# Two transformer blocks on one core: seven additions for one strided sum, operand tiles ahead of a weight split, and waits bank by bank

## The reference, cut to what matters

```python
def rms_norm(x, g):
    xf = x.astype(jnp.float32)
    y = xf * lax.rsqrt(jnp.mean(xf * xf, axis=-1, keepdims=True) + EPS)
    return (y * g.astype(jnp.float32)).astype(x.dtype)
...
    ca = memory_cross_attention(rms_norm(x, g_mem_pre[l]), m, ...)     # mem_q
    x = x + rms_norm(swiglu(rms_norm(x, g_ffn_pre[l]), ...), ...)      # ffn_up
...
    mix = dilated_attention_mixer(rms_norm_2(x, mixer_norm[layer]), ...)   # dil_in, dil_out
    x = x + mix
    x = x + conv_ffn(rms_norm_2(x, ffn_norm[layer]), ffn_w_up[layer], ...) # conv_up
```

## Time and profile before

| | us |
|---|---|
| median of 3 runs | 1588.36 |
| lowest and highest | 1587.85, 1592.78 |
| the profiled execution | 1588.06 |
| its span (first to last instruction) | 1586.2 |
| TensorE busy | 1538.0 (97%) |
| VectorE busy | 865.1 (55%) |
| ScalarE busy | 610.0 (38%) |
| GpSimd busy | 244.8 (15%) |

### The profile page before, as it was taken

One profiled execution on the slowest core, in us unless ns is written; L12 is line 12 of the kernel. 1 busy time (PEld: TensorE's weight loads), 2 busy tenths in 40 slices (PEclk: granted clock), 3 DMA queues, 4 the chain that ended last, 5 costly groups with the idle time before them and its releaser, 6 DMA issues.

```text
span 1586.2 us, 21184 instructions
## 1 busy us (share of the span) xinstructions
PE 1538.0 (97%) x7444; PEld 1270.7 (80%) x7444; DVE 865.1 (55%) x1135; ACT 610.0 (38%) x911; POOL 244.8 (15%) x273
## 2 busy tenths in 40 slices
PE   6999999999999999999999899999999999999998
PEld 4888777987887788888888678888997888888887
DVE  6213777436462743433423776747877766667323
ACT  6322433544234422222322643434765433334222
POOL 0010000014102400000000455645451100000000
PEclk9999999999999999999999999999999999999999
DMA  5343000431203133333223122232102232332331
GB/s 163 116 150 106 1 1 0 160 128 59 80 1 106 54 106 106 88 98 106 85 101 106 54 73 87 82 105 80 28 1 80 80 106 83 102 105 80 106 106 53
DMA packets 152797, 132.04 MB, mean 83 GB/s; under 512 B 6300, under 2 KB 137628, under 8 KB 152740
## 3 DMA queue, kind: packets, MB, share of 16 engines
q1 hardware_dynamic: 150836, 128.11, 26.3%
q0 software_dynamic: 848, 3.17, 0.6%
q10 hardware_dynamic: 1056, 0.00, 0.0%
HBM read 129.15 MB, written 2.12 MB: 83 GB/s over the span
## 4 chain that ended last, share of the span: by engine, by line
PE 89%; DVE 5%; ACT 2%; POOL 2%; issue 1%; DMA 0%; DVEq 0%; ACTq 0%; SPq 0%; POOLq 0%
PE ps L1715 25%; PE ps L1717 25%; PE ps L1716 25%; PE ps L1938 3%; PE ps L438 2%; PE ps L2048 1%; POOL x_t L743 1%; DVE work L1245 1%; PE ps L471 1%; DVE a_lo L1266 1%; PE ps L1926 1%; PE ps L573 1%; PE ps L1955 1%; PE ps L2035 1%; PE ps L1869 1%
## 5 line engine op out<-in xcount | busy, mean ns | idle before, releaser
L1715 PE MATMUL ps<-a_hi,w_hi 128*128 128x512 f32 (+2 forms) x1672 | 652.5, 390 | 15.9 <-DVE a_lo L1266 8.9
L1717 PE MATMUL ps<-a_hi,w_lo 128*128 128x512 f32 (+2 forms) x1672 | 646.6, 387 | 0.0
L1716 PE MATMUL ps<-a_lo,w_hi 128*128 128x512 f32 (+2 forms) x1672 | 646.4, 387 | 0.0
L1715 PEld LDWEIGHTS ps<-a_hi,w_hi 128*128 128x128 f32 (+1 forms) x1672 | 315.0, 188 | 88.0 <-DVE a_lo L1266 12.2
L1218 DVE TENSOR_TENSOR w_lo<-raw,w_hi 128x2048 fp32r<-128x2048 f32 x94 | 215.5, 2292 | 290.4 <-ACT w_hi L821 289.7
L1717 PEld LDWEIGHTS ps<-a_hi,w_lo 128*128 128x128 f32 (+1 forms) x1672 | 314.9, 188 | 64.5
L1716 PEld LDWEIGHTS ps<-a_lo,w_hi 128*128 128x128 f32 (+1 forms) x1672 | 315.1, 188 | 62.9 <-issue 0.7
L821 ACT ACTIVATE w_hi<-raw 128x2048 fp32r<-128x2048 f32 x118 | 225.8, 1913 | 303.0 <-PE ps L1717 301.5
L748 POOL TENSOR_TENSOR w_lo<-raw,w_hi 128x2048 fp32r<-128x2048 f32 x24 | 110.6, 4609 | 452.5 <-ACT w_hi L821 452.5
L1578 DVE TENSOR_TENSOR arena<-ps,rstd 128x512 f32<-128x512 f32 x88 | 60.1, 689 | 173.5 <-PE ps L1717 167.2
L1648 DVE RECIPROCAL rstd<-std 128x512 f32<-128x512 f32 x24 | 80.5, 3353 | 26.3 <-ACT std L1131 26.3
(11 more groups left out here) (217 smaller groups left out, 1503.6 us busy)
## 6 DMA issues: line engine op xcount, KB each, us to landing
raw<-in_w_gate_up SPq DMA_DIRECT2D x44, 512.0 KB, 4.7
raw<-in_ffn_w_up SPq DMA_DIRECT2D x44, 512.0 KB, 4.7
raw<-in_attn_w_in SPq DMA_DIRECT2D x36, 512.0 KB, 4.1
raw<-in_w_in SPq DMA_DIRECT2D x24, 512.0 KB, 4.7
raw<-in_w_down SPq DMA_DIRECT2D x22, 512.0 KB, 4.2
raw<-in_ffn_w_down SPq DMA_DIRECT2D x22, 512.0 KB, 4.2
raw<-in_w_mem_kv SPq DMA_DIRECT2D x16, 512.0 KB, 4.0
raw<-in_w_out SPq DMA_DIRECT2D x8, 512.0 KB, 4.0
```

The costliest lines, as they stand in the source:

```text
L1715: pe.matmul(dst, s_hi, m_hi, start=start, stop=False, skip_group_check=across)
L1716: pe.matmul(dst, s_hi, m_lo, start=False, stop=False, skip_group_check=across)
L1717: return pe.matmul(dst, s_lo, m_hi, start=False, stop=stop, skip_group_check=across)
```

## The change

- `invert_pre` (all four norms): the one reduction over 8 tiles of squares becomes seven additions into `square_sum`. Each waits for its tile of squares, and from the second on for the addition before it. TensorE waits for a count of 7 instead of 1.
- Ahead of conv_up, ScalarE waits for the end of dil_out, writes `a_hi` of tiles 4 and 5, splits the weights, writes `a_hi` of tiles 6 and 7, and only then makes the squares of tiles 4 to 7.
- `feature_major("conv_up", "")`: the wait for all banks on entering goes; the waits for each bank in `opening` stay.

```diff
+            def only_hi(name, ready, tiles):
+                for k in tiles:
+                    act.wait_ge(ready, k + 1)
+                    act.activation(a_hi[:, k, :], x_t[:, k, :], ACT.Identity, scale=vcol(name, k)).then_inc(norms[name].hi, 1)
+
+            def squared(name, k):
+                act.activation(x_squares[name][:, k, :], x_t[:, k, :], ACT.Square).then_inc(norms[name].sq, 1)
...
             over_chunks(act, G["dil_out"], wide, peel=1)
+            act.wait_ge(tile_done, G["dil_out"].signal_end)
+            only_hi("ffn_2", x_block2, (4, 5))
             split_hi(Chunk(G["conv_up"], 0, 2, 0))
-            gained_hi("ffn_2", x_block2, range(4, KT))
+            only_hi("ffn_2", x_block2, (6, 7))
+            for k in range(4, KT):
+                squared("ffn_2", k)
             rstd_out("ffn_2", "conv_up")
...
             def invert_pre(name):
 
-                dve.wait_ge(norms[name].sq, KT)
-                dve.tensor_reduce(square_sum, x_squares[name].rearrange("p k n -> p n k"), axis=AX.X, op=ALU.add)\
-                   .then_inc(norms[name].added, 1)
+                norm, of = norms[name], x_squares[name]
+                for k in range(1, KT):
+                    dve.wait_ge(norm.sq, k + 1)
+                    if k > 1:
+                        dve.wait_ge(norm.added, k - 1)
+                    dve.tensor_tensor(square_sum, of[:, 0, :] if k == 1 else square_sum, of[:, k, :], ALU.add)\
+                       .then_inc(norm.added, 1)
                 if name != "mixer_2":
                     invert(norms[name])
...
-                        pe.wait_ge(norm.added, 1)
+                        pe.wait_ge(norm.added, KT - 1)
...
-                            pe.wait_ge(norms["mixer_2"].added, 1)
+                            pe.wait_ge(norms["mixer_2"].added, KT - 1)
...
-            feature_major("conv_up", "dil_out", ready=norms["ffn_2"].ready, tail=1)
+            feature_major("conv_up", "", ready=norms["ffn_2"].ready, tail=1)
```

## The result

| | before | after |
|---|---|---|
| median, us | 1589.70 | 1596.72 |
| lowest and highest (14 runs each) | 1587.85, 1592.86 | 1592.64, 1603.32 |
| profiled execution, us | 1588.06 | 1597.63 |
| its span, us | 1586.2 | 1595.8 |
| its mean granted clock | 0.995 | 0.991 |

The ratio is 1.0044, with a 95% interval of 1.003 to 1.0058: the changed kernel is slower by 0.44%. The forecast was 1591.5 with a range up to 1595.0; the median lies above that range, and "within 0.3%", which had most of the chance, did not come.

A forecast was written before the change was run, and what follows sets the result against it. TensorE, busy 97% of the span, was taken to bound the kernel. Terms of 0, +2.1, +0.5 and +0.5 us (mem_q, ffn_up, dil_in, conv_up) gave +3.1 on the median of 1588.36: 1591.5 us, range 1586.6 to 1595.0.

The forecast's parts named there:

- within 0.3%: Whole kernel: the time can't be told from no change, 0.3% being about 4.8 us; chance 0.74.
- The order of service: VectorE and GpSimd: the engine that has waited longest is served, and an instruction keeps its turn to its end.
- ffn_up: +2.1: In ffn_up GpSimd's split holds the seventh addition, so L1869 starts at 542.0 instead of 539.89: +2.1 us.
- dil_in: +0.5: In dil_in the sum is early, but L1256 is held by GpSimd's split and broadcast L1898 starts later: +0.5 us.
- conv_up: the first chunk 1.5 earlier: In conv_up the first chunk ends 1.5 us earlier, but GpSimd's split precedes the seventh addition: +0.5 us for L1869.
- the rival of a won race: In conv_up the seventh addition is ahead of GpSimd, giving -1.5 there and 1589.5 us in all; chance 0.25.
- the one without blocking: VectorE keeps its turn between additions, or their pitch is 0.7: 1586.7 us; chance 0.12.
- The sum of 3.1: The place terms added: 0 in mem_q, 2.1 in ffn_up, 0.5 in dil_in, 0.5 in conv_up, +3.1 us.
- the three stalls that the forecast named: New TensorE stalls: 2.1 us in ffn_up, about 2.7 in dil_in, 2.0 in conv_up.
- The clock falls in a new stall: A new TensorE stall lowers the granted clock: 1593.5 to 1594.9, 1594.3 us; chance 0.21.
- One fall costs 2.0 to 3.4: Price in us of one clock fall, from the stretch 380 to 388 with granted clock 0.57.
- mem_q's 0: In mem_q the last addition asks at 396.25, before GpSimd's split at 396.83; not blocked, not waited for: 0 us.

The follow-up runs named there:

- GpSimd's wait in mem_q: The changed kernel, with GpSimd's weight split of mem_q's second chunk waiting for the sum of squares: 1592.43 us, ratio 1.0026.
- Parts 2 and 3: ScalarE's new order ahead of conv_up and the single bank waits, put into the kernel before with its strided sum kept: 1587.95 us, ratio 0.9996.
- a filled one in conv_up: The changed kernel, with nine unread matmuls ahead of TensorE's wait for the sum in mem_q, ffn_up and conv_up: 1593.11 us, ratio 1.0022.

## Why the prediction was wrong, step by step

**What was right.** The order of service and its price. ffn_up: +2.1 forecast, 2.02 measured. dil_in: +0.5 and 0.46, by the way forecast (the sum early, the diagonal held). conv_up: the first chunk 1.5 earlier (from ScalarE's restart to its second split 13.12 us before, 1233.32 - 1221.70 = 11.62 after), tile 6 the only stall (0.39, forecast 0.3), GpSimd 0.12 us ahead of the seventh addition (forecast 0.17), and +0.5 against 0.55. GpSimd was ahead in conv_up in each of the changed kernel's three profiles, so the rival of a won race is out, and so is the one without blocking.

**What failed first: the clock's place in the argument.** The sum of 3.1 put the clock at nothing; behind the stalls the account has 6.5 us of it, 4.8 of them behind the three stalls that the forecast named. The step is "The clock falls in a new stall", with 0.21, and there "One fall costs 2.0 to 3.4". Its mechanism was the real one. It failed twice. It asked whether one fall would come and priced one, though the forecast itself opened three stalls and named them; there was one behind each of them, and behind a fourth. And the only row on which the price stood, 380 to 388 at 0.57, is two falls in one: a single one loses 1.7 us of clock and moved what follows by 1.3 to 2.0. With the right count and price the same sum would have been 3.1 + 3 x 1.6 = 7.9, so 1596.3; measured were 1596.7. This is worked out afterwards, mem_q and the fall near 892 don't stand in it, and that the two agree so well is in part luck: beside the changed kernel the kernel before took 1589.70 and not 1588.36, so that the loss measured is 7.0 us.

The row of the profile that argued against a fall was 892 to 896, busy 1.34 of 4 and 1.00 granted. One such stretch said that idling doesn't always bring a fall. That is true (ffn_up, above), but it isn't the same as rarely, and in the changed kernel the clock did fall near there (892 to 898), just ahead of that wait.

**What failed second: mem_q's 0.** The step read that the last addition asks at 396.25 and GpSimd at 396.83, a margin of 0.58 us, and took it for sure, with no bound. But GpSimd's start followed from an opening that the clock had slowed in this execution; the earlier trace rows show that slow opening, and I didn't put the two together. Without it the split comes 1 us earlier and wins. It costs 2.06 us of stall and a fall behind it; taking it away gave 3.97 us between two matched profiles, and 4.3 by the medians or 2.9 by the ratios (GpSimd's wait in mem_q).

**The parts of the change.** Parts 2 and 3 do what they say and are worth 1.5 us on TensorE, which the held sum of conv_up takes back; alone they are within what can be measured (0.9996). The additions carry the loss, and not by being seven: with one operand in PSUM the same seven lose nothing (0.9983, of which 0.1% is the order's).

## What to carry to other kernels

Before a VectorE instruction with one SBUF operand is replaced by several with two, look at which GpSimd instruction starts within their stretch: the last one can be held for all of it, and a margin of half a microsecond read from one profile is no margin where the start on the other side hangs on the clock. A running sum in PSUM avoids it, as does a wait on GpSimd's side where nobody waits for GpSimd. And where TensorE is busy for 97%, price a new stall of 2 us with the fall that can follow it, once for each stall: here 1.3 to 2.0 us on top, with a chance that the profiles at hand must give, since it was 14 in 18 behind the held instructions and 6 in 13 at another place.

## What was not expected of the hardware

- A stall of TensorE of 1.9 to 2.7 us was followed by a fall of the granted clock to 1.2 GHz in 14 of the 18 cases of the last table; a filled one in conv_up was not. Each fall loses the same 1.7 us of clock. But a wait of 2.0 us ahead of the transposes had a fall behind it in only 6 of 13 profiles.
- An addition with an operand in PSUM and one with both in SBUF take the same 0.69 us when free, so the way around the hold-up costs VectorE nothing.
- Whether an instruction was held in mem_q went with the clock lost in the opening ahead of it: 3.4 us lost, and GpSimd started too late to hold it; less, and it was held. That the clock is the cause is argued. This may be one source of the changed kernel's spread (1592.6 to 1603.3, before 1587.9 to 1592.9), though not the only one: with GpSimd's wait in mem_q it still reached 1599.5. The spread goes with the clock: the two fastest runs of the changed kernel (1592.6) have a mean granted clock of 0.995, the slowest (1603.3) one of 0.987.
